# A fixed number of constant products on TensorE ahead of seven waits in two attention mixers

## What is computed

```
x = x + 0.5 * swiglu(rms_norm(x, g_ffn1), w1_gate, w1_up, w1_down)      # D_FF = 2816
proj = rms_norm(x, g_mix) @ w_in                                       # first mixer
y_a = dsa_attention(rope(q_a), rope(k_a), v_a, rope(q_idx), rope(k_idx), w_idx, w_uv_a, top_k)
    # index scores, top-k mask, softmax, values of 128 latent columns, expanded by w_uv
y_b = stick_breaking_attention(q_b, k_b, v_b)                          # 8 heads
    # z = q k; log_not = log_sigmoid(-z); between = reversed cumsum; a = exp(...); o = a v
x = x + (sigmoid(gate_a) * (y_a @ w_o_a) + sigmoid(gate_b) * (y_b @ w_o_b)) @ w_out
x = x + 0.5 * swiglu(rms_norm(x, g_ffn2), w2_gate, w2_up, w2_down)

x = x + hybrid_mixer(rms_norm_2(x, norm1_w))                           # second mixer
    # half of it an mLSTM, half a differential attention (softmax p0 - lam * softmax p1)
x = x + hierarchical_moe(rms_norm_2(x, norm2_w))                       # 32 experts, 2 per token
```

## Time and profile before

| | us |
|---|---|
| median of 3 executions | 2007.29 |
| lowest and highest of them | 1999.26, 2008.22 |
| the profiled execution, its own time | 2006.74 |
| its span, from the first to the last instruction | 2004.8 |
| outside the span | 1.9 |

### The profile page before, as it was taken

One profiled execution on the slowest core, in us unless ns is written; L12 is line 12 of the kernel. 1 busy time (PEld: TensorE's weight loads), 2 busy tenths in 40 slices (PEclk: granted clock), 3 DMA queues, 4 the chain that ended last, 5 costly groups with the idle time before them and its releaser, 6 DMA issues.

```text
span 2004.8 us, 21910 instructions
## 1 busy us (share of the span) xinstructions
PE 1913.8 (95%) x8782; PEld 1382.0 (69%) x8782; DVE 1044.9 (52%) x1690; ACT 700.1 (35%) x1139; POOL 42.2 (2%) x67
## 2 busy tenths in 40 slices
PE   7999999998999979999999999999999999999998
PEld 6888888875778857888888888877666444443443
DVE  5443544467667886544434447565765333433333
ACT  5321332345555355432222324475642111111111
POOL 0000000100000001000000000000000000000000
PEclk9999999998899999999999999999989999999999
DMA  6323334134223304333333323221259999999997
GB/s 176 98 84 105 95 100 111 51 77 53 73 63 69 103 18 133 102 96 96 93 97 99 101 76 109 79 64 53 64 215 354 421 420 420 420 421 420 421 421 287
DMA packets 256301, 338.65 MB, mean 169 GB/s; under 512 B 10000, under 2 KB 218896, under 8 KB 232640
## 3 DMA queue, kind: packets, MB, share of 16 engines
q1 hardware_dynamic: 249744, 320.71, 46.8%
q0 software_dynamic: 5872, 15.41, 2.1%
q10 hardware_dynamic: 576, 1.05, 0.1%
HBM read 332.74 MB, written 8.39 MB: 170 GB/s over the span
## 4 chain that ended last, share of the span: by engine, by line
PE 75%; DVE 10%; DMA 9%; ACT 5%; issue 1%; SPq 1%; DVEq 0%; ACTq 0%
PE bank L183 74%; DMA large<-w_up 8%; PE bank L186 1%; ACT wH L189 1%; ACT p L189 1%; DVE PTL L195 1%; DVE y L195 1%; SPq L225 1%; DVE p L198 1%; ACT T L189 1%; DVE score L201 0%; DVE st L207 0%; DMA stage<-w_gate 0%; DVE cv L201 0%; DVE score L219 0%
## 5 line engine op out<-in xcount | busy, mean ns | idle before, releaser
L183 PE MATMUL bank<-hH,wH 128*128 128x512 f32 x1096 | 435.7, 398 | 15.9 <-DVE stage0L L195 11.6
L183 PE MATMUL bank<-hL,wH 128*128 128x512 f32 x1096 | 429.3, 392 | 0.0
L189 ACT ACTIVATE wH<-stage 128x1024 fp32r<-128x1024 f32 (+3 forms) x231 | 228.4, 999 | 98.0 <-PE bank L183 84.1
L183 PE MATMUL bank<-large,xF 128*64 128x512 f32 x1024 | 237.8, 607 | 17.3 <-DMA large<-w_up 15.4
L183 PEld LDWEIGHTS bank<-hH,wH 128*128 128x128 f32 x1096 | 207.9, 190 | 62.1 <-DVE stage0L L195 11.6
L183 PEld LDWEIGHTS bank<-hL,wH 128*128 128x128 f32 x1096 | 208.0, 190 | 43.7 <-issue 1.7
L183 PEld LDWEIGHTS bank<-large,xF 128*64 128x64 f32 x1024 | 75.2, 139 | 150.1 <-issue 142.6
L183 PE MATMUL bank<-hidH,wH 128*128 128x512 f32 x352 | 137.5, 390 | 2.1 <-DVE stage2L L195 0.9
L183 PE MATMUL bank<-hidL,wH 128*128 128x512 f32 x352 | 137.0, 389 | 0.0
L195 DVE TENSOR_TENSOR yoL<-bank,yoH 64x512 fp32r<-64x512 f32 x64 | 44.1, 689 | 148.5 <-ACT yoH L189 147.5
L183 PE MATMUL bank<-large,hF 128*64 128x512 f32 x512 | 115.9, 595 | 0.0
(11 more groups left out here) (494 smaller groups left out, 3356.7 us busy)
## 6 DMA issues: line engine op xcount, KB each, us to landing
large<-w_gate SPq DMA_DIRECT2D x64, 1024.0 KB, 27.0
large<-w_up SPq DMA_DIRECT2D x64, 1024.0 KB, 26.8
large<-w_down SPq DMA_DIRECT2D x64, 1024.0 KB, 26.9
stage<-w_in SPq DMA_DIRECT2D x56, 512.0 KB, 4.1
stage<-w_gate SPq DMA_DIRECT2D x44, 512.0 KB, 3.8
stage<-w_up SPq DMA_DIRECT2D x44, 512.0 KB, 3.9
stage<-w_down SPq DMA_DIRECT2D x16, 512.0 KB, 3.6
stage<-w_out SPq DMA_DIRECT2D x12, 512.0 KB, 4.0
```

Of the source, the lines that this page charges most:

```text
L183: return self.e.matmul(*a, **k) if self.e is not None else Nothing()
L189: return self.e.activation(*a, **k) if self.e is not None else Nothing()
```

## The change

A new helper on TensorE, `keep_clock(use, count)`. If its count is not zero it waits until the bank is free, and then does that many products of constants into the bank: `rident` by the first four matrices of `rmats`, 512 columns each. The step's own products follow after its own waits and begin with `start=True`, so they overwrite what the constants left. The counts are fixed in the code, for seven places: `chunk_turn` of query chunk 1 (6), `b1` of heads 0, 2 and 6 (9, 7, 9), `expand` of group 0 (13), `dvalues` of head 2 (6), `out_half` of tile 0 (7). These are 57 products. Nothing else is moved, on any engine.

```
+            def keep_clock(use, count):
+
+                if count:
+                    free(use)
+                    pe.wait_ge(*after("operands",))
+                for _ in range(count):
+                    pe.matmul(use.t[:, :], rident[:, :], rmats[:, 0:4, :].rearrange("p a b -> p (a b)"), start=True, stop=True, skip_group_check=True)
...
             def chunk_turn(s):
                 if s.rope:
+                    keep_clock(s.bank3, {("qa", 1): 6}.get(s.key, 0))
...
                     elif s.kind == "expand":
+                        keep_clock(s.banks[0], {0: 13}.get(n, 0))
                         pe.wait_ge(*after("ol", n))
...
                     elif s.kind == "b1":
+                        keep_clock(s.z[0], {0: 9, 2: 7, 6: 9}.get(n, 0))
                         pe.wait_ge(*after("kb_zero", n % 2))
...
             def out_half(s):
 
+                if s.ready and s.m == 0:
+                    keep_clock(s.bank, 7)
                 pe.wait_ge(*after("w_lo", s.units[1].i))
...
                     elif s.kind == "dvalues":
+                        keep_clock(s.bank, {2: 6}.get(n, 0))
                         pe.wait_ge(*after("dpt", 4 * n + 3))
```

## The result

The changed kernel takes 1993.8 us (median of 6, 1989.92 to 1994.85), the kernel before 2003.53 us beside it (median of 6, 1999.26 to 2008.22). The ratio is 0.9938, with a 95% interval of 0.9925 to 0.9952, so 0.6% faster, against a forecast of 1993.5 us. The profiled execution of the changed kernel took 1993.76 us, with a span of 1991.9 us and a mean granted clock of 0.992 (before: 2004.8 us and 0.981).

The account below looks back on a forecast made before the run. TensorE carries 75% of the chain of waits and runs at half speed in seven stretches. Savings of 1.7 + 3.4 + 3.2 + 1.7 + 2.1 + 0.7 + 1.0 = 13.8 us gave 1993.5 us, range 1988 to 2001.

Parts of the forecast that it names:

- The bound: Seven stretches of TensorE at the lower clock, six after idle waits for VectorE; ending them saves 13.8 us in sum.
- The price of the constants: At all seven places: fillers end before the operand comes, with 0.4 to 1.3 us over, so they cost nothing.
- b1: Slow stretches behind heads 0, 2 and 6: half the busy time saved, 1.7, 3.4 and 3.2 us, all passing.
- dvalues: Slow stretch there: 3.4 us saved on TensorE, 2.1 passes, 1.3 turns idle as transposes at 1472.44 wait for VectorE's `p`.
- out_half: Slow stretch there: 1.7 us saved, all passing, since the chain stays on TensorE for 27.12 us.
- expand: Slow stretch there: 0.7 us saved of 3.3, from VectorE's 0.72 us wait before `PTL`; ends 0 and 3.3.
- The sign named for it: Behind 706 us, after `expand`, more short idle pieces should appear in the profile after.
- chunk_turn: Clock already down there; joined work brings it back sooner: gain 1.0 us, between a loss of 0.8 and a gain of 1.4.
- The first rival: Savings run into other waits, and low stretches remain and may grow: 6 us gained, 2001 us; chance 0.20.
- The gate: DMA's stream of the experts last waits for TensorE's chain at about 1537 us; gains before it reach the end in full.

Follow-up runs that it names:

- the two kernels with a delay: The changed kernel with 22 more constants (5.0 us) ahead of the first expert's transposes, or of expert 10's: ratio 0.9948 and 0.9941.

## Why the prediction was right

**The bound.** The slow stretches cost in sum what they were said to: the seven sites gave 13.8 us, the sum forecast. Its terms are off by -0.5 to +1.1 us each and cancel.

**The price of the constants.** Nothing, as forecast: 0.23 us apiece at the full clock, beside waits that were longer. Doubling them shows what they cost without the cover.

**b1.** 1.55, 3.0 and 2.8 against 1.7, 3.4 and 3.2. Half of the busy time was a little too much. By the granted clock of the stretch, busy time by (1 - PEclk), head 0 gives 3.40 x 0.46 = 1.56, head 2 6.71 x 0.48 = 3.2, head 6 6.38 x 0.48 = 3.1, which is nearer. No other wait appeared behind them.

**dvalues.** 1.9 against 2.1, but the wait is not where the prediction put it. It had the transposes of 1472.44 (1460.29 after) wait for `p`. In the changed kernel `p` ends at 1459.21 + 0.75 = 1459.96, and TensorE is in unbroken work from 1457.21 to the transposes and beyond: they follow the product of 1460.06 at its usual distance of 0.23 us. What a faster TensorE ran into is VectorE's `xT`, 4.6 us behind the start of `dvalues`:

```profile
1456.25 1.12 PE L183 MATMUL bank<-sq,mats 128*128 128x512 f32 x2 [1.00 <-DVE xT L195]
...
1459.21 0.75 DVE L201 SCALAR_TENSOR_TENSOR p<-p,st,p 128x512 f32<-128x512 f32 x1
...
1460.06 0.39 PE L183 MATMUL bank<-hmH,stage3L 128*128 128x512 f32 x1
1460.29 0.60 PE L186 MATMUL bank<-mats,p 128*128 128x128 f32 x4
```

`xT` starts 3.9 us behind `dvalues` in both kernels (1465.75 and 1455.51), so up to `sq` only 0.35 us are won, and 1.00 turns into idle time; from `sq` to the transposes 1.55 are won. That VectorE takes a part was foreseen, and 1.3 us of idle time too; that the size came so near from the wrong wait is luck.

**out_half.** 1.2 against 1.7, since the low stretch at 1504.5 lies behind it in the same stretch. In eight other profiles with constants there, without it, the stretch takes 35.3 us, and the site is worth 1.6.

**expand** is the term that was mis-sized: 0.7 forecast, 1.8 measured. The step counted one pause of VectorE, the 0.72 us before `PTL`. The timeline of VectorE in the kernel before shows two more behind that wait, and in the changed kernel they are shorter or gone:

```profile
707.45 1.25 DVE L195 TENSOR_TENSOR yaL<-bank,yaH 64x128 fp32r<-64x128 f32 x4 [1.41 <-ACT yaH L189]
...
709.58 0.76 DVE L207 TENSOR_REDUCE st<-bank 128x1 f32<-128x256 f32 x2 [0.37 <-PE bank L183]
```

```profile
698.09 1.25 DVE L195 TENSOR_TENSOR yaL<-bank,yaH 64x128 fp32r<-64x128 f32 x4 [1.02 <-ACT yaH L189]
...
699.78 0.74 DVE L207 TENSOR_REDUCE st<-bank 128x1 f32<-128x256 f32 x2
```

That is 0.39, 0.37 and 0.72 us, 1.5 in all. The wait put down to ScalarE's `yaH` is TensorE's in the end, since `yaH` is read from the bank that the slow products fill. The sign named for it came: behind `expand` TensorE is now busy for 5.83 of 6.90 us, for 6.60 of 6.80 before. A pause has to be followed back to its origin before it is called another engine's.

**chunk_turn.** 1.6 against 1.0. The mechanism was the one described: the constants join the work, and the clock comes back sooner. VectorE's pauses of 0.75 us (before `sq`) and 0.77 and 0.64 (behind it) become none, 0.36 and 0.30. The loss of up to 0.8 us that was set against it didn't come. The product that was at 463.70 stands at 464.12, but its place against `sq` is the same (6.39 before, 6.40 after).

**The other stretches** were forecast at nothing and give -0.9 in sum. The first rival, low stretches elsewhere, is there in part: 0.5 us behind `expand`, 1.7 us between `ge` and `xF`. It is not what decides.

**The gate.** Over the change as a whole the shift at `oh` (13.4 us) reaches the end (12.9). The standstill of DMA is still there, but in this profile it lies 5 us behind the products of the table (1524.04), and not before them:

```profile
1521.70:1524.20 2.50, 0.24 (x3) 0.17 (x2) 2.04 (x8) 0.00 (x0) 0.00 (x0) 1.00 0.56 128
1528.90:1530.10 1.20, 1.20 (x9) 0.73 (x7) 1.10 (x4) 0.00 (x0) 1.07 (x1) 1.00 0.00 0
```

In the second profile of the changed kernel it lies before them, as in the earlier trace rows: 16 GB/s from 1521.3 to 1523.8, with `ge` at 1523.66. It goes with the low stretches: ahead of `ge` where one lies between `oh` and `ge`, behind it where one lies 6 us ahead of `oh`. So which product of TensorE the stream waits for is a draw as well, and a delay of 5.0 us there passed in part only.

**The level.** The forecast took the kernel before at 2007.3, and further executions put its median at 2003.5 beside the changed kernel and at 2005.7 to 2006.7 in the other comparisons. By the ratio, 0.62% of 2005.7 are 12.4 us. That the sum met the time to 0.3 us is partly luck: each profile is a draw, the one before had lost at all seven sites, and an execution of it that keeps the clock at some of them has less to gain.

## What to carry to other kernels

Before an idle TensorE is left alone, look at the granted clock behind its waits. Where a wait of 1.8 us or more is followed by a slow stretch, filler products shorter than the wait cost nothing and save that stretch, here 1.2 to 3.0 us a site in an execution that has it (8 of 12 unfilled waits here). The filler must be shorter than the shortest wait that the place can have, since its excess is paid in full. What it wins is kept only where the next operand isn't another engine's, so follow the work to the next wait before counting it.

## What the runs showed of the hardware

- The same wait, in the same program or one that differs far away from it, may or may not be followed by a low clock: waits of 2.27, 2.34 and 2.82 us stood without a fall in some profiles and with one in others. 25 executions of the kernel before lay from 1999.2 to 2013.7 us, and their mean clocks from 0.988 down to 0.979, in the main the slower the lower.
- The clock also fell where TensorE had not been idle: at 1504.5, behind products of one column and of 36 and at the start of a row of transposes. The rows of the changed kernel show no idle time there:

```profile
1502.22 1.05 PE L183 MATMUL bank<-mats,acc 128*128 128x1 f32 x8
...
1503.54 1.11 PE L183 MATMUL bank<-router_fold,J 128*128 128x36 f32 x8
1504.46 4.92 PE L186 MATMUL bank<-mats,xT 128*128 128x128 f32 x28
```

  In the second profile of the same kernel the same 28 transposes, at 1504.51, took 3.25 us at the full clock.

- The 128x128 transposes of a constant hold the clock as well as products of 512 columns: 1.00 behind all six sites with either.
- Open: why the time from `xF` to the end differs by up to 3.0 us (446.05 to 449.04, without the two kernels with a delay) although DMA moves 420 GB/s throughout; and what decides, at waits near 1.8 us, whether the clock falls.
